# Input embedding projected directly behind the sums of the feed-forward norms, banks exchanged, and the third mixer's input split into a place of its own

## The chip, the core and the metric

The kernel runs on one core of a Trainium2 chip. The metric is the device time of one execution in microseconds (us). The core's engines are TensorE (PE, matmuls; its weight loads are listed as PEld), VectorE (DVE), ScalarE (ACT), GpSimd (POOL) and SyncE (SP, which here only issues DMAs). Each engine runs its own instructions in order and waits for others by semaphores.

## The reference

Two blocks follow each other on 512 tokens of width 1024. All is fp32. The first block has two layers; the second also has two (several small mixers, a gated merge), and the change touches it only by one wait. Of the first block:

```
for i in range(DEPTH):                       # DEPTH = 2
    y = mixer_ab(x, ...) if i % 2 == 0 else mixer_c(x, ...)
    x = layer_norm(ALPHA * x + y, ln_mix_g[i], ln_mix_b[i])
    f = conv_ffn(x, ffn_w_gate[i], ffn_w_up[i], ffn_conv_w[i], ffn_conv_b[i], ffn_w_down[i])
    x = layer_norm(ALPHA * x + f, ln_ffn_g[i], ln_ffn_b[i])
    x = x + jax.nn.sigmoid(x @ ple_w_gate[i]) * (p[i] @ ple_w_proj[i])
```

`conv_ffn` is `(gelu(conv3(x @ w_gate)) * (x @ w_up)) @ w_down` with an inner width of 2816 (22 tiles of 128). `p[i]` is a second input (an embedding) of width 256 for each layer; "embedding" below means it. `mixer_c` computes values, queries and keys from x and a differential attention.

## The kernel before, in words

**Layout.** Activations stand transposed: a tile is 128 features by 512 tokens, x has eight tiles. A matmul of fp32 precision is made of three passes of a faster type: each operand is split into `hi` (rounded) and `lo` (the rest), and the passes are hi*hi, hi*lo, lo*hi (function `passes`, L719 to L721). ACT (or DVE) makes `hi`, DVE makes `lo` (`upper`, `lower`); the split input of the projection at work stands in `moving`. Sums over features (norms) are fp32 matmuls with a matrix of ones (L924 to L937).

**Weights.** All weights come as 375 blocks of 128 x 1024 in a fixed order (`block_plan`). SP loads them into a ring of two slots, POOL splits each half block into `w_hi` and `w_lo` (L2526, L2529) as soon as PE has used the same half of the block two places before (`half_done`, `block_done`), and PE waits for `split_ready`. A block is 24 matmuls of 512 columns.

**Order.** The order of every engine is written out by hand: lists of stages (`mixer_a`, `heads_ab`, ..., `residual_norm`, `feed_forward`, `per_layer`, `mixer_c`, ...) that run alike on each engine. Norms are numbered i = 0 to 3; even ones follow a mixer, odd ones the feed-forward. Eight PSUM banks of 512 columns hold all results of PE; each stage has its banks by number.

**The steps that matter here.**
- Setup: DVE makes the angles for the rotary tables, ACT computes Sin of them (L1529 to L1531), and only then, in its `mixer_a`, copies the first values from banks 0 to 3 (L1434). PE's latent blocks go to the same banks and wait for these copies. ACT copies the latent blocks behind DVE's last setup step (L1541).
- A norm (`residual_norm` on PE, `norm_squares` on ACT, `residual`, `norm` on DVE): ACT squares each tile, DVE adds the squares (L2067, `add_squares`), PE sums mean (L927) and squares (L932). DVE centres four tiles (L2131) and POOL four (`recentre`, L2551); DVE scales each tile into a bank (L2160), ACT writes `hi` (L1609), DVE `lo` (L2137). At the end DVE computes x = hi + lo for all eight tiles (L2168).
- `feed_forward`: PE computes gate and up of the first tile pairwise as the normed tiles arrive, then tile by tile. DVE starts with the split of the embedding (`lower(("p", layer))`), then per tile two taps of the convolution (L2181, L2185), the product (L2190) and the `lo` of the hidden tile (L2195). Then PE computes the down projection in two halves, for which DVE and ACT have little to do.
- `per_layer`: PE projects the first half of the embedding (`project_p`, banks 4 to 7) when the four centred tiles and the mean are through with their banks, then the first two gate blocks pairwise as the normed tiles arrive, then gate blocks 2 to 7 to banks n % 4, and the embedding's second half in between. ACT takes the sigmoid (L1635), DVE multiplies in the bank (L2203) and adds to x (L2205). In layer 0 ACT and DVE then split all eight tiles of x into `moving` (L1429, L1842) for `mixer_c`; in layer 1 they make `gained` for the second block tile by tile.
- `mixer_c`: values of four 128-token groups in two halves (banks 0 to 3, then 4 to 7), then 16 query and key blocks in banks t % 4.

## Time and profile before

| | |
|---|---|
| median of 3 runs | 2528.85 us (2526.66 to 2528.97) |
| the profiled execution's own time | 2527.82 us |
| its span, first to last instruction | 2526.0 us |
| mean granted TensorE clock | 0.987 |
| PE busy | 2424.8 us (96%) |
| POOL busy | 1898.6 us (75%) |
| DVE busy | 1149.5 us (46%) |
| ACT busy | 690.9 us (27%) |
| weights and inputs read | 203.71 MB, 81 GB/s over the span |

Busy time is the time in which an engine had an instruction at work. Matmuls overlap each other, so their own durations (0.39 us) are longer than the distance of their starts. The granted clock is given in parts of full speed. In a timeline row stand the start, the duration, the engine, the line, the operation with out<-in, and in brackets how long the engine had been idle before and who released it; rows of equal instructions in a stretch are merged with their count.

### The profile page before, as it was taken

What the parts mean: (1) busy time and instruction counts of PE and PEld (TensorE: products, weight loads), DVE (VectorE), ACT (ScalarE), POOL (GpSimd) and SP (SyncE); (2) the same over time, 40 slices, a digit from 0 to 9 for tenths busy, and PEclk for the clock granted to TensorE, in tenths of its full rate; (3) what the DMA queues carried; (4) which work ended last, traced back from release to release, by engine and by line L of the source; (5) the groups of instructions that cost most, each with busy time, mean ns of one, the idle gap of its engine ahead of it and who ended that gap; (6) DMA issues with size and microseconds to landing.
All of it is one profiled execution on the core that took longest, in us unless ns stands there. A gap on an engine that the chain in (4) does not pass through costs nothing.

```text
span 2526.0 us, 32296 instructions
## 1 busy us (share of the span) xinstructions
PE 2424.8 (96%) x11118; PEld 1871.2 (74%) x11118; DVE 1149.5 (46%) x1587; ACT 690.9 (27%) x1242; POOL 1898.6 (75%) x1553
## 2 busy tenths in 40 slices
PE   7989989999999999899999999999999999999998
PEld 6755768888877843678888777767888877678886
DVE  6576563330261477643322474555322645553323
ACT  2166233330021157233320133144010231450101
POOL 8703578888877753698888799735999998359995
PEclk9999999999999999999999999999999999999999
DMA  4201122222222210122222232201222222112222
GB/s 175 84 9 43 51 75 100 98 93 100 92 75 100 85 41 1 67 100 91 100 97 95 75 113 100 84 34 59 100 97 94 92 100 85 41 53 99 99 99 84
DMA packets 57547, 207.11 MB, mean 82 GB/s; under 512 B 6512, under 2 KB 6896, under 8 KB 57200
## 3 DMA queue, kind: packets, MB, share of 16 engines
q1 hardware_dynamic: 55872, 199.87, 22.2%
q10 hardware_dynamic: 1584, 5.96, 0.6%
q8 instruction: 65, 1.06, 0.2%
q14 instruction: 26, 0.21, 0.0%
HBM read 203.71 MB, written 2.10 MB: 81 GB/s over the span
## 4 chain that ended last, share of the span: by engine, by line
PE 76%; DVE 10%; POOL 7%; issue 4%; ACT 2%; DMA 1%; POOLq 0%; DVEq 0%; ACTq 0%; SPq 0%
PE bank L719 21%; PE bank L721 20%; PE bank L720 20%; POOL w_hi L2526 4%; PE bank L813 4%; PE bank L768 3%; POOL w_lo L2529 3%; PE bank L841 2%; PE bank L867 2%; PE bank L888 1%; DVE branch_lo L1842 1%; DVE moving_lo L1842 1%; DVE x L2168 1%; DVE work L1882 1%; PE bank L906 1%
## 5 line engine op out<-in xcount | busy, mean ns | idle before, releaser
L2526 POOL TENSOR_TENSOR w_hi<-ring,unit 128x512 fp32r<-128x512 f32 x750 | 846.4, 1129 | 497.3 <-PE bank L721 357.0
L2529 POOL TENSOR_TENSOR w_lo<-ring,w_hi 128x512 fp32r<-128x512 f32 x750 | 1010.6, 1347 | 58.7
L719 PE MATMUL bank<-moving_hi,w_hi 128*128 128x512 f32 x1962 | 776.3, 396 | 26.8 <-DVE moving_lo L2137 12.3
L721 PE MATMUL bank<-moving_hi,w_lo 128*128 128x512 f32 x1962 | 768.8, 392 | 0.0
L720 PE MATMUL bank<-moving_lo,w_hi 128*128 128x512 f32 x1962 | 768.7, 392 | 0.0
L719 PEld LDWEIGHTS bank<-moving_hi,w_hi 128*128 128x128 f32 x1962 | 371.5, 189 | 116.9 <-issue 25.7
L720 PEld LDWEIGHTS bank<-moving_lo,w_hi 128*128 128x128 f32 x1962 | 371.4, 189 | 78.8 <-issue 1.9
L721 PEld LDWEIGHTS bank<-moving_hi,w_lo 128*128 128x128 f32 x1962 | 371.1, 189 | 78.4
L2473 DVE TENSOR_TENSOR region<-region,bank 128x512 f32<-128x512 f32 x64 | 39.7, 682 | 278.4 <-PE bank L721 278.4
L719 PE MATMUL bank<-hid_hi,w_hi 128*128 (+1 forms) x352 | 137.7, 391 | 0.0
L1780 ACT ACTIVATE region<-bank 128x512 f32<-128x512 f32 x64 | 38.1, 598 | 363.4 <-PE bank L721 363.4
L721 PE MATMUL bank<-hid_hi,w_lo 128*128 (+1 forms) x352 | 137.0, 389 | 0.0
L720 PE MATMUL bank<-hid_lo,w_hi 128*128 (+1 forms) x352 | 137.0, 389 | 0.0
L813 PE MATMUL bank<-region 64*128 64x512 f32 (+3 forms) x448 | 125.4, 574 | 11.8 <-ACT work L1496 3.0
L1903 DVE TENSOR_REDUCE negmax<-bank 128x2 f32<-128x256 f32 (+2 forms) x64 | 59.1, 924 | 112.6 <-PE bank L817 87.1
L2181 DVE SCALAR_TENSOR_TENSOR region<-bank,cols,region 128x511 f32<-128x511 f32 x44 | 32.9, 748 | 162.6 <-ACT region L1623 162.6
L1448 ACT ACTIVATE region<-bank 128x1024 f32<-128x1024 f32 (+2 forms) x80 | 66.7, 834 | 120.6 <-PE bank L867 120.4
L813 PEld LDWEIGHTS bank<-region 64*128 64x128 f32 (+1 forms) x448 | 40.1, 186 | 67.6 <-issue 46.5
L1599 ACT ACTIVATE region<-region 128x512 f32<-128x512 f32 x14 | 8.8, 631 | 265.5 <-DVE region L2059 183.6
L2091 DVE SCALAR_TENSOR_TENSOR region<-x,bank 128x512 f32<-128x512 f32 x18 | 12.2, 687 | 150.4 <-PE bank L721 150.2
L867 PE MATMUL bank<-tabs,work 128*128 128x128 f32 x496 | 69.5, 276 | 9.3 <-DVE work L1882 7.2
L867 PEld LDWEIGHTS bank<-tabs,work 128*128 128x128 f32 x496 | 53.9, 141 | 32.9 <-issue 25.8
(299 smaller groups left out, 3441.1 us busy)
## 6 DMA issues: line engine op xcount, KB each, us to landing
ring<-in_weights SPq DMA_DIRECT2D x375, 512.0 KB, 3.2
x<-in_x_t ACTq DMA_DIRECT2D x4, 512.0 KB, 8.4
out<-region SPq DMA_DIRECT2D x8, 256.0 KB, 2.2
region<-in_tables ACTq DMA_DIRECT2D x1, 1312.0 KB, 9.3
region<-in_tables ACTq DMA_DIRECT2D x1, 1024.0 KB, 5.7
region<-in_p_t ACTq DMA_DIRECT2D x2, 512.0 KB, 4.9
region<-in_tables SPq DMA_DIRECT2D x1, 320.0 KB, 10.4
small_w<-in_small_w ACTq DMA_DIRECT2D x1, 320.0 KB, 5.9
```

The lines of the kernel that those rows point to most:

```text
L719: pe.matmul(bank, lhs[0], rhs[0], start=start, stop=False, skip_group_check=True)
L720: pe.matmul(bank, lhs[0], rhs[1], start=False, stop=False, skip_group_check=True)
L721: return pe.matmul(bank, lhs[1], rhs[0], start=False, stop=stop, skip_group_check=True)
L768: mm = pe.matmul(bank, cols_of(w, k * P, P)[p == 2], moved(k)[p == 1], start=(j == 0), stop=(j == 23), skip_group_check=True)
L813: mm = pe.matmul(at[c], q(u, c)[:, i * P:i * P + P], k(u, c)[:, 0:w], start=True, stop=True)
L841: mm = pe.matmul(out_bank(u)[HD * c:HD * c + HD, 2 * P * h + lo:2 * P * h + 2 * P], v(u, t, c), pt_half[:, h, c, t, lo:2 * P], start=(open ...
L867: mm = pe.transpose(psum[4 + c][:, kt * P:kt * P + P], prob[:, 2 * (t % 2) + c, kt * P:kt * P + P], ident)
L1448: act.activation(pt_half[:, i // 2, :, 0:kt, lo:lo + P], banks[:, 4:6, 0:kt * P].rearrange("p c (k q) -> p c k q", k=kt), ACT.Copy).then_i ...
L1842: dve.tensor_tensor(pair[1], src, pair[0].bitcast(F32), ALU.subtract).then_inc(parts_ready, 1)
L1903: dve.tensor_reduce(negmax[:, at:at + 2], banks[:, b:b + 2, 0:w], AX_X, ALU.max, negate=True).then_inc(maxed, 2)
L2526: pool.tensor_tensor(w_parts[0][:, s, at], ring[:, s, at], unit[:, 0:1].broadcast_to([P, BLK // 2]), ALU.mult).then_inc(split_hi, 1)
L2529: pool.tensor_tensor(w_parts[1][:, s, at], ring[:, s, at], w_parts[0][:, s, at].bitcast(F32), ALU.subtract).then_inc(split_ready, 1)
```

## The change

It has these parts.
- ACT's four copies of the first values stand in `setup`, before the wait for DVE's angles.
- x = hi + lo becomes `join_parts`. Odd norms keep it at their end. Behind even norms it moves to the end of DVE's `feed_forward`, behind the last hidden tile, followed by the split of the embedding, which stood at its beginning. A new semaphore `x_joined` holds back ACT's scaled tiles and DVE's residual of the odd norm.
- Odd norms: DVE adds the squares of tiles 0 to 5; tiles 6 and 7 are added by PE with a matmul of their own each.
- `project_p` stands before the waits for the centred tiles; the embedding goes to banks 4, 6, 0, 1 (before 4 to 7) and the gate to 5, 7, 2, 3 (before 0 to 3). The gate pair also waits for the variance. The second block's first projection waits for the seventh finished tile of x (before: the fifth sigmoid).
- `mixer_c` reads `moving_c`, two places of 16 KB a partition in memory that is free then. In layer 0 ACT makes `hi` of tile n-1 behind the sigmoid of tile n, and DVE `lo` of tile n-1 behind the sum of tile n. The value halves use banks 4 to 7 first (when six tiles of x are finished) and 0 to 3 then; the first four query blocks use banks 6, 7, 2, 3.

```diff
+PLE_BANK, GATE_BANK = (4, 6, 0, 1), (5, 7, 2, 3)
+SQUARES_ODD = 6
+C_BANK = (6, 7, 2, 3) + (0, 1, 2, 3) * 3
...
+        moving_c = parts("moving_c", 32, KD, S)
...
             # PE, residual_norm
                 if i % 2:
-                    pe.wait_ge(square_added, T["square_added"][(i, KD - 1)])
-                mm = pe.matmul(psum[7][:], ones, square_sum, start=True, stop=(i % 2 == 1), skip_group_check=True)
-                if i % 2 == 0:
-                    pe.wait_ge(squared, T["squared"][("ln", i, KD - 1)])
-                    mm = pe.matmul(psum[7][:], ones, square_late[:, 3, :], start=False, stop=True, skip_group_check=True)
+                    pe.wait_ge(square_added, T["square_added"][(i, SQUARES_ODD - 1)])
+                pe.matmul(psum[7][:], ones, square_sum, start=True, stop=False, skip_group_check=True)
+                for n in range(SQUARES_ODD if i % 2 else KD - 1, KD):
+                    pe.wait_ge(squared, T["squared"][("ln", i, n)])
+                    mm = pe.matmul(psum[7][:], ones, square_late[:, n - 4, :], start=False, stop=(n == KD - 1),
+                                   skip_group_check=True)
...
             # PE, per_layer
+                        project_p(layer, 0)
                         pe.wait_ge(centered, CENTRED * (2 * layer + 2))
                         pe.wait_ge(drift_ready, 2 * layer + 2)
-                        project_p(layer, 0)
-                        project_pair(AT[("plegate", layer, 0)], (psum[0][:], psum[1][:]), ("ln", 2 * layer + 1))
+                        pe.wait_ge(variance, 2 * layer + 2)
+                        project_pair(AT[("plegate", layer, 0)], [psum[GATE_BANK[j]][:] for j in range(2)],
+                                     ("ln", 2 * layer + 1))
...
             # PE, mixer_c
-                    pe.wait_ge(x_ple, KD)
-                    tokens_values([("vC", 4 * half + i) for i in range(4)], moved,
-                                  [psum[4 * half + i][:] for i in range(4)], S, 2, ready=("x", 1))
+                    pe.wait_ge(x_ple, KD if half else KD - 2)
+                    tokens_values([("vC", 4 * half + i) for i in range(4)], moved_c,
+                                  [psum[4 * (1 - half) + i][:] for i in range(4)], S, 2, ready=("x", 1))
...
             # PE, project_second
-                    pe.wait_ge(ple_sig, KD * DEPTH - KD + 5)
+                    pe.wait_ge(x_ple, KD * DEPTH - KD + 7)
...
             # ACT, setup (and gone from mixer_a)
+                values(range(4), ("vA", 3), lambda i: v_ab[:, i, :], lambda i: psum[i])
                 act.wait_ge(setup_dve, SETUP["rest"])
...
             # ACT, per_layer
-                    if layer and n:
-                        gain(0, n - 1)
+                    if n:
+                        gain(0, n - 1) if layer else upper_x(n - 1)
...
-                    for n in range(KD):
-                        act.wait_ge(x_ple, n + 1)
-                        upper(("x", 1, n), moving[0][:, n, :], x[:, n, :])
+            def upper_x(n):
+                act.wait_ge(x_ple, n + 1)
+                upper(("x", 1, n), moving_c[0][:, n, :], x[:, n, :])
...
             # DVE, residual
-                    for n in range(4, KD):
+                    for n in range(4, SQUARES_ODD):
                         add_squares(i, n)
...
             # DVE, norm
-                dve.wait_ge(parts_ready, T["parts"][("ln", i, KD - 1)])
+                if i % 2:
+                    dve.wait_ge(parts_ready, T["parts"][("ln", i, KD - 1)])
+                    join_parts()
+
+            def join_parts():
                 for n in range(KD):
                     hi, lo = both(moving, np.s_[:, n, :])
-                    dve.tensor_tensor(x[:, n, :], hi.bitcast(F32), lo.bitcast(F32), ALU.add)
+                    ins = dve.tensor_tensor(x[:, n, :], hi.bitcast(F32), lo.bitcast(F32), ALU.add)
+                return ins
...
             # DVE, feed_forward
-                lower(("p", layer), both(p_parts, np.s_[:, :, :]), p_in_t)
                 with dve.Fori(0, KF // 2) as it:
...
+                join_parts().then_inc(x_joined, 1)
+                lower(("p", layer), both(p_parts, np.s_[:, :, :]), p_in_t)
...
             # DVE, per_layer
+                    if layer == 0 and n:
+                        lower_x(n - 1)
                 if layer:
                     last_gained(0)
-                for n in range(KD if layer == 0 else 0):
-                    lower(("x", 1, n), both(moving, np.s_[:, n, :]), x[:, n, :])
+                else:
+                    lower_x(KD - 1)
+
+            def lower_x(n):
+                lower(("x", 1, n), both(moving_c, np.s_[:, n, :]), x[:, n, :])
```

## Rows read from the trace of the kernel before

**Rows 1.** page, part 1: busy time (share of the span) and instructions of each engine

```profile
PE 2424.8 (96%) x11118; PEld 1871.2 (74%) x11118; DVE 1149.5 (46%) x1587; ACT 690.9 (27%) x1242; POOL 1898.6 (75%) x1553
```

**Rows 2.** waits of PE over the span: total, times, longest us

```profile
PE bank L719 <- DVE moving_lo L1842: 14.6, 4, 9.6
```

**Rows 3.** windows by stretch: length, busy of PE, PEld, DVE, ACT, POOL, granted clock, DMA

```profile
701.67:706.50 4.83, 4.83 (x12) 3.78 (x13) 4.60 (x8) 1.50 (x3) 0.00 (x0) 0.50 0.00 0
...
721.00:760.00 39.00, 38.73 (x167) 31.30 (x168) 14.52 (x18) 3.59 (x6) 37.75 (x32) 1.00 0.29 100
```

**Rows 4.** timeline of PE, first value block's end: start, us, engine, line, [idle before]

```profile
37.95 0.76 PE L719 MATMUL bank<-moving_hi,w_hi 128*128 128x512 f32 x1 [3.65 <-ACT region L1434]
...
44.84 0.39 PE L719 MATMUL bank<-moving_hi,w_hi 128*128 128x512 f32 x1
```

**Rows 5.** timeline of ACT, setup and first latent copy

```profile
33.75 0.63 ACT L1529 ACTIVATE rope_a<-region 128x512 f32<-128x512 f32 x1 [17.09 <-DVE region L1945]
...
46.83 0.60 ACT L1541 ACTIVATE region<-bank 128x512 f32<-128x512 f32 x1 [7.52 <-DVE cmp_bias_bf L1969]
```

**Rows 6.** timeline of POOL, setup

```profile
33.25 1.61 POOL L2529 TENSOR_TENSOR w_lo<-ring,w_hi 128x512 fp32r<-128x512 f32 x1
```

**Rows 7.** timeline of PE, start of the feed-forward behind norm 0

```profile
339.82 0.42 PE L719 MATMUL bank<-moving_hi,w_hi 128*128 128x512 f32 x1
...
353.36 0.49 PE L719 MATMUL bank<-moving_hi,w_hi 128*128 128x512 f32 x1 [1.22 <-DVE region L2190]
```

**Rows 8.** timeline of DVE, the same stretch and the down projection's end

```profile
336.34 11.57 DVE L2168 TENSOR_TENSOR x<-moving_hi,moving_lo 128x512 f32<-128x512 f32 x8
347.84 2.31 DVE L1842 TENSOR_TENSOR p_lo<-region,p_hi 128x1024 fp32r<-128x1024 f32 x1
...
631.11 1.29 DVE L2091 SCALAR_TENSOR_TENSOR region<-x,bank 128x512 f32<-128x512 f32 x2 [56.83 <-PE bank L721]
```

**Rows 9.** timeline of POOL: beside the sums, and in the down projection

```profile
339.58 1.49 POOL L2526 TENSOR_TENSOR w_hi<-ring,unit 128x512 fp32r<-128x512 f32 x1
341.15 1.63 POOL L2529 TENSOR_TENSOR w_lo<-ring,w_hi 128x512 fp32r<-128x512 f32 x1
...
560.43 1.04 POOL L2526 TENSOR_TENSOR w_hi<-ring,unit 128x512 fp32r<-128x512 f32 x1 [0.31 <-PE bank L721]
561.55 1.30 POOL L2529 TENSOR_TENSOR w_lo<-ring,w_hi 128x512 fp32r<-128x512 f32 x1
```

**Rows 10.** timeline of DVE, feed-forward norms 1 and 3

```profile
692.48 5.32 DVE L2067 TENSOR_TENSOR region<-region 128x512 f32<-128x512 f32 x4
...
703.25 1.42 DVE L2160 SCALAR_TENSOR_TENSOR bank<-region,cols,rstd 128x512 f32<-128x512 f32 x2
...
714.83 1.60 DVE L2137 SCALAR_TENSOR_TENSOR moving_lo<-bank,cols,moving_hi 128x512 fp32r<-128x512 f32 x2
...
1447.78 1.59 DVE L2137 SCALAR_TENSOR_TENSOR moving_lo<-bank,cols,moving_hi 128x512 fp32r<-128x512 f32 x2
```

**Rows 11.** timeline of PE, feed-forward norms 1 and 3

```profile
697.85 1.12 PE L932 MATMUL bank<-region,tabs 128*128 128x512 f32 x2 [2.58 <-DVE region L2067]
...
701.67 0.76 PE L719 MATMUL bank<-p_hi,w_hi 128*128 128x512 f32 x1 [2.69 <-issue]
...
709.87 0.47 PE L719 MATMUL bank<-moving_hi,w_hi 128*128 128x512 f32 x1 [0.20 <-POOL w_lo L2529]
...
730.16 0.39 PE L719 MATMUL bank<-moving_hi,w_hi 128*128 128x512 f32 x1
...
1463.89 0.39 PE L719 MATMUL bank<-moving_hi,w_hi 128*128 128x512 f32 x1
```

**Rows 12.** timeline of POOL, recentring in norm 1

```profile
695.98 5.40 POOL L2551 TENSOR_TENSOR region<-region 128x512 f32<-128x512 f32 x4 [1.35 <-ACT region L1601]
```

**Rows 13.** timeline of PE, first value block of the third mixer

```profile
764.20 0.52 PE L719 MATMUL bank<-w_hi,moving_hi 128*128 128x512 f32 x1 [3.77 <-DVE moving_lo L1842]
...
767.92 0.39 PE L719 MATMUL bank<-w_hi,moving_hi 128*128 128x512 f32 x1
```

35 lines of the change are left out of this document (21 added, 14 removed).

## The prediction, written before the changed kernel was run

> **What bounds the kernel now.** The first part of the page has TensorE (PE) busy 96% of the span [rows 1]: the matmuls set the end, and a change pays only where PE stands still or runs slowly. So I read next where PE stood (the waits of PE over the span, then PE's timeline around each wait). PE's largest releaser is the DVE split into `moving_lo`: 14.6 us in four waits, one of them inside the part that changes [rows 2]. A stop costs more than its length: behind the stop of 697.85 to 701.67 the granted clock is 0.50 (the 1.2 GHz level) for 4.83 us, while in 721 to 760 it is 1.00 (2.4 GHz) [rows 3]. At full clock matmuls start 0.227 us apart (0.68 for the three passes), at half clock 0.427; a block of 24 is 5.44 us of PE. GpSimd (POOL) splits each half block in about 2.4 us when alone, 2.72 us of PE each; it is the second bound wherever it starts late.
>
> **Change 1, the first value copies ahead of the Sin work.** Before, PE stands 3.65 us from 34.30 to 37.95, and reaches the next block at 44.84, 6.89 us later for 5.44 us of work, since the first matmuls are cold [rows 4]. ACT sat 17.09 us waiting for DVE's angles, ran Sin, and only then copied [rows 5]. With the copies first, they start at 34.34, and one takes 0.60 us (as the ACT copy at 46.83 [rows 5]), so the first ends at about 34.95 and PE starts at 35.1. The weights' first half is split at 34.86 [rows 6], so that is no bound. A gap of 0.95 us I take as harmless: behind the 1.22 us gap of [rows 7] the next matmuls are at full pace. PE reaches the next block at 35.1 + 5.44 = 40.6; POOL's next two halves, 2.4 to 3.1 each [rows 9], are there at 39.7 to 41.1. I take 40.7: gain 44.84 - 40.7 = **4.1**. Price: Sin starts at 36.6 + 1.3 (table load) instead of 33.75, so DVE's tables end some 4 us later and ACT's first latent copy moves from 46.83 [rows 5] to about 50.7; PE needs it only at the fifth latent block, 35.1 + 4 x 5.44 = 56.9. Bounds: 4.9 (the whole stop and its cold part) and 2.5 (POOL, already the pace here, meets DVE's moved work and gives 1.6 of it back).
>
> **Change 2, the sum x = hi + lo leaves the start of the feed-forward.** Behind norms 0 and 2 DVE runs the eight sums (11.57 us) and the split of p (2.31 us) before its first convolution step [rows 8]. That does two things to PE: it reaches the third tile only at 353.36 behind DVE's late product, and POOL's halves stretch to 3.14 us (1.49 + 1.62 and the gaps) against 2.42 alone [rows 9], which stops PE for 0.3 to 0.4 us three times. From 339.82 to 353.36 are 13.54 us for 48 matmuls, 10.88 at full pace [rows 7]: 2.66 lost. Without the sums the first product is there at 344.9 (341.6 when ACT's first tap ends, two taps 1.8, Gelu 0.65, product 0.7) and PE asks for it at 350.7; POOL's halves fit. Norm 2 has the same rows. Gain 2 x 2.66 = **5.3**; below, 2 x 1.2 (the DVE wait alone).
> The sums now run behind DVE's last hidden tile, in the down projection, where DVE idles 56.83 us before the residual [rows 8] and POOL waits for PE 0.31 us before each half [rows 9]. With two slots of two halves, POOL finishes a half 3 x 2.72 - 2.42 = 5.7 us ahead of its need. 13.9 us of sums and split delay it by 4.4 halves x (3.14 - 2.72) = 1.9 us, under 5.7: cost 0. ACT's scaled tiles and DVE's residual wait for it, both needed some 40 us later. If that lead were gone, 2 x 1.9.
> The Trainium skill (SBUF — State Buffer, Who interferes with whom) has the port between DVE and GpSimd as an exclusive lock, also for a DVE instruction with two SBUF inputs: the second to come fully blocks. The sums have two SBUF inputs and both engines do stretch, but POOL by 0.45 and 0.33 us a piece, not by a whole DVE instruction of 0.65. By the rule taken whole, POOL would lose 9 to 10 x 0.65 = 6.5 us in the down projection, 0.8 more than its lead, and the sum would be 1.6 us smaller.
>
> **Change 3, feed-forward norms (1 and 3).** Of DVE's four adds of squares (5.32 us [rows 10]) two go to PE as two more matmuls of 0.9 us. The squares' sum then follows the mean's matmuls at 695.3 without the 2.58 us stop [rows 11] and ends at 698.0 instead of 698.95, so the norm's chain comes 0.9 earlier. `project_p` no longer waits for centring (its stop of 2.69, named issue, ends 0.1 behind DVE's last centre): it runs from 698.0 to 703.6, warm, in place of 701.67 to 709.5. POOL's four recentres end at 701.4 [rows 12] and its next half at 704.1, so the pair of gates starts with the first normed tile at 704.6. Now DVE paces it: its chain from the first scaled tile to the last `moving_lo` is 13.2 us (703.25 to 716.43) at norm 1 and 12.3 at norm 3 (ending 1449.37) [rows 10]; with 0.9 off and 0.4 to 0.6 on (POOL now splits beside the last tiles) the last is ready at 715.9 and 1449.1, and PE is through 1.6 us later, at 717.5 and 1450.6, where before it was at 709.87 + 48 x 0.227 = 720.8 and at 1455.2. Then POOL is the pace for three halves, since its first half can start only behind the sixth tile, and the sums stand beside more of them. By halves of 3.14 PE reaches the fourth gate's second half at 726.2 and 1459.05, before at 730.16 and 1463.89 [rows 11]: gains 3.9 and 4.8, **8.7**. Above: 5.8 each (2.7 stop, 2.0 cold, 0.9, 0.2). Below: 2 each, the cold part alone; the clock rival goes under that.
>
> **Change 4, third mixer's input to its own place.** The splits could not start before the last gate block had read `moving`; PE stood 3.77 us and ran nine matmuls cold [rows 13]. Its fourth group of three starts at 767.92; at full pace it would have been there at 762.3 (764.20 less 3.77 of stop and 0.16 of drain, and three groups of 0.68): 5.6. Now seven of eight tiles are split under the gate blocks. The last block ends at 760.2; tile 7 takes sigmoid, product, sum, hi, lo: about 4 us, and is asked for by the fourth value block, 16.3 us later. The first half of the values also waits for six finished tiles (banks 4 to 7); the sixth is 5 us old by then. Gain **5.6**; below 3, if ACT's order (hi of tile n-1 between two sigmoids) delays a sigmoid. Each `lower` has two SBUF inputs and costs POOL 0.35 to 0.45; per block POOL has 5.44 - 4.8 = 0.6 to spare, just enough: **-0.3** at the start, where it has no lead (0 to -1). The wait of layer 1's first projection moves from the fifth sigmoid to the seventh finished tile, about 3 us before PE is there: 0. The exchanged banks of the queries wait for copies that are ten microseconds old: 0.
>
> **Sum.** 4.1 + 5.3 + 8.7 + 5.6 - 0.3 = 23.4 us. The profiled execution took 2527.8 (span 2526.0), within the measured 2526.7 to 2529.0 and 1 below the median: 2527.8 - 23.4 = 2504.4.
>
> **Rivals.**
> A, the freed time goes to the port: POOL, starting at once behind the recentres, meets every DVE step of the norm, and at each norm the tile-paced pair gives back 1 us and the three halves behind it 2; the start gives back 1.6, mixer C 2: 9.6 together, gain 13.8, 2514. For: POOL is the releaser in [rows 11] already. Against: the same two halves stood beside the same tiles before, only later.
> B, slower: the clock stays low through the norms. In place of one long stop PE now has many short ones, and a stop of 2.58 and one of 2.69 with 1.12 of work between [rows 11] brought it to 0.50 [rows 3]. If projection and pair (72 matmuls) run at 0.427 us, they end at 698.0 + 10.2 + 20.5 = 728.7, 7.9 behind before, at both norms: -15.8 instead of +8.7, total -1.1 (2528.9); each further cold matmul adds 0.2, and with 20 of them the loss is over 0.2%. It decides if the pair's gaps (1.45 to 1.7 us a tile for 1.36 us of work) are enough to lower the clock. Against: in 339 to 353 PE stopped 0.3 to 1.2 us four times and the starts keep 0.23.
> The Trainium skill (TensorE: Matmul & The Clock Gate, A second HAM failure mode: psum-queue depth-cycling) reports just this, short idle times between groups of matmuls making the clock swing. By that rule the pairs would run between the levels; rival B is its full price, half of it 2516.
> C, mixer C's stop is only moved: a wait for the sixth or eighth finished tile ends late and the clock falls again. Gain 17.8, 2510.
>
> **Chances.** Forecast with its own spread 0.72, A 0.12, C 0.08, B in part (2514 to 2524) 0.05, B whole 0.03. 0.2% is 5 us, what this measurement can tell from no change. Faster 0.95, same 0.03, slower 0.02. The terms' bounds give gains up to 27.6 (2500) and down to 10 to 14 (2514); the range for 8 in 10 is 2499 to 2513.
>
> **What would show it.** No PE wait of 3.65 near 34; the third tile of each feed-forward without a wait for DVE's product, and the `x` sums some 40 us before the residual, with no PE wait beside them; six instead of two instructions in the squares' sum, `p_hi` matmuls right behind at clock 1.00; PE waits of 0.1 to 0.4 us on `moving_lo` of the norm in the pair; no wait and clock 1.00 at the first value block of mixer C. Wrong: clock 0.5 in the pair (B), waits on `w_lo` over 3 us more than before (A), a wait over 1 us at mixer C's start (C).

## The result and the profile after

The changed kernel takes 2511.9 us (median of 6 runs, 2511.1 to 2514.5) where the kernel before takes 2529.4 (6 runs, 2526.7 to 2530.9): a ratio of 0.9935, 95% interval 0.9924 to 0.9945, so 0.55 to 0.76% faster. The forecast was 2504.4, its range 2499 to 2513. The profiled execution of the changed kernel has a span of 2511.0 against 2526.0: 15.0 us less, where the forecast counted 23.4.

The first part of the page: TensorE does the same work, and eight matmuls more for the squares, in a shorter span [rows 1].

```profile
span 2511.0 us, 32310 instructions
PE 2426.7 (97%) x11126; PEld 1874.6 (75%) x11126; DVE 1164.7 (46%) x1583; ACT 691.3 (28%) x1242; POOL 1899.4 (76%) x1553
```

The waits of PE over the whole span:

```profile
PE bank L724 <- DVE moving_lo L2153: 17.4, 4, 6.2
PE bank L724 <- DVE moving_lo L1856: 10.9, 3, 9.7
...
PE bank L724 <- DVE x L2228: 1.6, 1, 1.6
```

Of a wait, the profile gives the total, the number and the longest one. The four waits for `moving_lo` that were 14.6 us [rows 2] are three and 10.9: mixer C's is gone. But the split inside the norms (12.3 us in two waits before, norms 0 and 2) now stops PE four times, and the wait for `x` is new. PE's timeline at the places of [rows 4, 7, 11, 13]:

```profile
35.19 0.47 PE L724 MATMUL bank<-moving_hi,w_hi 128*128 128x512 f32 x1 [0.73 <-ACT region L1443]
40.74 0.39 PE L724 MATMUL bank<-moving_hi,w_hi 128*128 128x512 f32 x1
...
348.40 0.39 PE L724 MATMUL bank<-moving_hi,w_hi 128*128 128x512 f32 x1
...
692.44 0.79 PE L724 MATMUL bank<-p_hi,w_hi 128*128 128x512 f32 x1
...
701.15 0.47 PE L724 MATMUL bank<-moving_hi,w_hi 128*128 128x512 f32 x1 [2.55 <-DVE moving_lo L2153]
...
704.75 0.51 PE L724 MATMUL bank<-moving_hi,w_hi 128*128 128x512 f32 x1
...
723.58 0.40 PE L724 MATMUL bank<-moving_hi,w_hi 128*128 128x512 f32 x1
...
755.26 0.39 PE L724 MATMUL bank<-w_hi,moving_c_hi 128*128 128x512 f32 x1
...
1446.94 0.40 PE L724 MATMUL bank<-moving_hi,w_hi 128*128 128x512 f32 x1
...
1456.37 0.50 PE L724 MATMUL bank<-p_hi,w_hi 128*128 128x512 f32 x1 [1.62 <-DVE x L2228]
...
1483.61 0.50 PE L724 MATMUL bank<-gained_hi,w_hi 128*128 128x512 f32 x1 [0.27 <-DVE gained_lo L2304]
```

Both kernels issue the same 2834 groups of three passes in the same order, so the n-th group of one can be set against the n-th of the other. How far the changed kernel is ahead at each: 4.1 us at 40.74 (before 44.84, [rows 4]), 5.0 at 348.40 (353.36, [rows 7]), 5.1 at the end of the down projection, 7.3 at 723.58, 12.7 at 755.26 (767.92, [rows 13]), 15.5 behind the next feed-forward's start, 17.6 at 1446.94, 16.0 at 1456.37, 15.1 near the end. The difference of two such numbers is what a stretch gained, whatever happened ahead of it. By it the start gave 4.2, the two feed-forward starts with the norms ahead of them 2.1 and 1.9 (the part behind the pair of gates 2.7 each time), norms 1 and 3 gave 2.2 and 2.1, mixer C 5.6. The wait for `x` took 1.7, and stretches that nobody had edited took 1.1 (heads A, the first mixer's attention) and gave 1.0 (heads C, the third mixer's). The second block took 0.8. Of that, 0.5 stands at 1483.61, where its first projection now waits for DVE's `gained_lo`; the forecast had priced this place at 0.

The same division is used for every run below. Each number is how much later (+) or earlier (-) the stretch ends than in the changed kernel, its own start taken off; the last column is the sum over the whole kernel, with the stretches that the table leaves out.

| kernel | norm 0 and start of gates | norm 1 | second `p`, layer 0 | mixer C start | heads C | norm 2 and start of gates | norm 3 | second `p`, layer 1 | all |
|---|---|---|---|---|---|---|---|---|---|
| before | +2.1 | +2.2 | -0.2 | +5.6 | +1.0 | +1.9 | +2.1 | -1.7 | +15.1 |
| e14 changed again | -0.1 | 0.0 | 0.0 | 0.0 | 0.0 | 0.0 | 0.0 | 0.0 | -0.3 |
| e1 POOL holds | -0.4 | +0.4 | -0.2 | 0.0 | +0.9 | -0.7 | +1.2 | -1.7 | -1.7 |
| e2 project_p late | -0.3 | -1.0 | 0.0 | 0.0 | 0.0 | -1.3 | +0.4 | -1.9 | -4.2 |
| e3 kept busy | -0.7 | -1.3 | +1.8 | 0.0 | +0.9 | -1.1 | -1.3 | +3.1 | -2.0 |
| e4 sums split | -0.1 | -0.7 | +0.1 | 0.0 | 0.0 | -1.3 | -1.7 | -0.6 | -3.9 |
| e6 sums back | +1.8 | -1.3 | +1.8 | 0.0 | +1.7 | +1.5 | -1.3 | +3.1 | +6.8 |
| e7 late and split | 0.0 | -1.7 | +0.1 | 0.0 | +1.7 | -0.1 | -1.8 | -0.7 | -2.2 |
| e9 mixer C back | -0.2 | 0.0 | 0.0 | +6.9 | +0.1 | -0.1 | 0.0 | 0.0 | +6.3 |
| e10 squares back | 0.0 | +0.7 | 0.0 | 0.0 | +0.9 | -0.7 | -1.0 | +3.1 | +2.0 |
| e11 neither | -0.8 | +1.9 | -0.2 | 0.0 | 0.0 | -1.1 | +1.9 | -1.9 | -1.4 |
| e12 late, even busy | -2.1 | +0.7 | -0.2 | 0.0 | 0.0 | -2.3 | +1.2 | -1.7 | -7.4 |
| e13 late, all busy | -2.1 | -1.0 | 0.0 | 0.0 | +1.7 | -2.3 | -1.0 | 0.0 | -5.3 |

The two profiled executions of the changed kernel (the first and e14, 2512.8 and 2512.5 us) differ by 0.1 at most in each stretch. Different kernels differ by 0.7 to 1.3 at norm 2 and by 0.9 or 1.7 in heads C though nothing was edited there, and by up to 3.0 in the second block, which the table leaves out (e3 and e12 gained 3.0 and 2.8 there): that much is not the edits' doing. Each row is also one execution of several. Those of e7 and e6 that were profiled took 2510.6 and 2519.6, about 3 and 2 us more than most of their others; e12's, at 2505.5, took 2 to 3.6 less than its others. So a row tells where that execution gained or lost, and its last column is no better measure of a kernel than the median.

**What stands at norm 1 now.** DVE's timeline, then POOL's:

```profile
697.29 3.06 DVE L2176 SCALAR_TENSOR_TENSOR bank<-region,cols,rstd 128x512 f32<-128x512 f32 x2
700.27 0.74 DVE L2153 SCALAR_TENSOR_TENSOR moving_lo<-bank,cols,moving_hi 128x512 fp32r<-128x512 f32 x1
...
710.82 12.46 DVE L2188 TENSOR_TENSOR x<-moving_hi,moving_lo 128x512 f32<-128x512 f32 x8
```

```profile
695.94 1.04 POOL L2554 TENSOR_TENSOR w_hi<-ring,unit 128x512 fp32r<-128x512 f32 x1
697.06 1.29 POOL L2557 TENSOR_TENSOR w_lo<-ring,w_hi 128x512 fp32r<-128x512 f32 x1
698.68 1.12 POOL L2554 TENSOR_TENSOR w_hi<-ring,unit 128x512 fp32r<-128x512 f32 x1 [0.33 <-PE bank L726]
699.88 1.60 POOL L2557 TENSOR_TENSOR w_lo<-ring,w_hi 128x512 fp32r<-128x512 f32 x1
```

DVE's first two scaled tiles took 3.06 us where they had taken 1.42 [rows 10]. The granted clock behind the stop of 698.60 to 701.15 (the columns are those of [rows 3], the last but two the clock):

```profile
702.00:704.00 2.00, 2.00 (x6) 1.54 (x6) 1.97 (x4) 1.18 (x2) 0.00 (x0) 0.50 0.65 223
704.00:706.00 2.00, 2.00 (x8) 1.63 (x7) 1.93 (x4) 0.89 (x2) 0.00 (x0) 0.75 0.10 39
```

The pair's first nine matmuls take 3.60 us (701.15 to 704.75) instead of 9 x 0.227 = 2.04; seven of them start 0.43 apart. ("Cold" below means matmuls at the lower of the two clock levels, granted clock 0.50, 1.2 GHz; "warm" means 1.00, 2.4 GHz.) Not all of these 1.6 us are the clock's. In e6 below, the same pair starts behind the same stop and stays warm, and its first nine take 2.40 (702.78 to 705.18): the clock costs 1.2. At the end of the pair the changed kernel has gained 2.1 us, where the forecast had 3.3 (717.5 against 720.8). With the pair warm it is 2.9 (e3 and e6).

**The sums behind norm 3.** Before, and now:

```profile
1449.41 7.69 DVE L2168 TENSOR_TENSOR x<-moving_hi,moving_lo 128x512 f32<-128x512 f32 x8
```

```profile
1434.17 12.46 DVE L2188 TENSOR_TENSOR x<-moving_hi,moving_lo 128x512 f32<-128x512 f32 x8
```

With the lead of 15.5 us added, the changed kernel's start in the same place (1449.7), but take 4.8 us more, since POOL now splits beside every one of them: a sum takes 0.69 us alone and 1.34 to 1.77 there. The finished tiles of `x` stand behind them. Among the kernels with eight sums in a row, PE waits for `x` in layer 1 exactly where the sums took 12.5 to 12.6 (the changed kernel, e3, e6, e9, e10, e13, e14) and nowhere that they took 7.7 or 9.6 (before, e1, e2, e11, e12).

### The profile page after: what moved, and what is told of

It is laid out like the page before. It is cut to its first block, busy times and chain, and to the rows that moved or that the text cites. A ratio compares the mean times of both kernels' runs of the same rounds, so it can differ in the third digit from the quotient of the medians.

```text
span 2511.0 us, 32310 instructions
## 1 busy us (share of the span) xinstructions
PE 2426.7 (97%) x11126; PEld 1874.6 (75%) x11126; DVE 1164.7 (46%) x1583; ACT 691.3 (28%) x1242; POOL 1899.4 (76%) x1553
## 4 chain that ended last, share of the span: by engine, by line
PE 81%; DVE 9%; POOL 5%; issue 3%; ACT 1%; DMA 0%; POOLq 0%; DVEq 0%; ACTq 0%
PE bank L724 22%; PE bank L726 22%; PE bank L725 22%; PE bank L818 4%; PE bank L773 3%; POOL w_hi L2554 3%; POOL w_lo L2557 2%; PE bank L846 2%; PE bank L872 2%; PE bank L893 1%; DVE branch_lo L1856 1%; DVE work L1896 1%; PE bank L911 1%; DVE negmax L1917 1%; ACT region L1707 0%
## 5 line engine op out<-in xcount | busy, mean ns | idle before, releaser
L724 PE MATMUL bank<-moving_hi,w_hi 128*128 128x512 f32 x1834 | 728.6, 397 | 24.1 <-DVE moving_lo L2153 17.4
L725 PE MATMUL bank<-moving_lo,w_hi 128*128 128x512 f32 x1834 | 721.5, 393 | 0.0
L726 PE MATMUL bank<-moving_hi,w_lo 128*128 128x512 f32 x1834 | 721.4, 393 | 0.0
L724 PEld LDWEIGHTS bank<-moving_hi,w_hi 128*128 128x128 f32 x1834 | 348.9, 190 | 106.8 <-issue 27.6
L725 PEld LDWEIGHTS bank<-moving_lo,w_hi 128*128 128x128 f32 x1834 | 349.1, 190 | 74.5 <-issue 1.9
L726 PEld LDWEIGHTS bank<-moving_hi,w_lo 128*128 128x128 f32 x1834 | 348.7, 190 | 73.9
L1469 ACT ACTIVATE work<-bank,negmax 128x512 f32<-128x512 f32 (+3 forms) x128 | 71.3, 565 | 24.7 <-DVE negmax L1917 24.7
L2215 DVE TENSOR_TENSOR hid_lo<-region,hid_hi 128x512 f32 x44 | 58.6, 1331 | 40.9 <-ACT hid_hi L1642 40.9
```

What stands on the lines that cost most here:

```text
L724: pe.matmul(bank, lhs[0], rhs[0], start=start, stop=False, skip_group_check=True)
L725: pe.matmul(bank, lhs[0], rhs[1], start=False, stop=False, skip_group_check=True)
L726: return pe.matmul(bank, lhs[1], rhs[0], start=False, stop=stop, skip_group_check=True)
L1469: act.activation(p, p if masked else psum[2 * (t % 2) + c][:, 0:w], ACT.Exp, bias=negmax[:, at:at + 1], scale=-1.0 if masked else 1.0, acc ...
L2215: dve.tensor_tensor(hid[1][:, tile, :], gelu_t[:, par, :], hid[0][:, tile, :].bitcast(F32), ALU.subtract).then_inc(hid_parts, 1)
```

## The experiments

Medians are of all runs of a kernel; before, in the same turns, was at 2527.6 to 2529.6 in the four sets.

### e1: is it POOL that holds DVE's first scaled tiles?

```diff
                 for n in range(CENTRED, KD):
                     pool.tensor_tensor(tiles[:, n, :], tiles[:, n, :], drift, ALU.subtract).then_inc(recentered, 1)
+                if i % 2:
+                    pool.wait_ge(normed, T["normed"][("ln", i, 1)])
```

> The changed kernel, but in norms 1 and 3 POOL waits, behind its four recentres, until DVE's first two scaled tiles are out, instead of splitting the next half block at once. Theory (the port): the two scaled tiles took 3.06 us instead of 1.42 because they stood behind POOL's w_lo and w_hi splits; with POOL still they take 1.4 us again and the first moving_lo is ready 1.5 us earlier. PE gains next to nothing by it (0 to 0.5 us a norm), since its pair then waits for POOL's half, which comes at 698.8 + 2.4 = 701.2 instead: the wait ahead of the pair stays 2.5 us and changes its releaser from DVE to POOL. Rival (PSUM or PE): the tiles are slow because PE's matmuls of project_p write other banks at the same time; then they still take 3 us with POOL still, and the pair starts about where it did.

Measured: 2511.1 us (one run). DVE's, POOL's and PE's timeline at norm 1 of this kernel:

```profile
696.11 1.42 DVE L2176 SCALAR_TENSOR_TENSOR bank<-region,cols,rstd 128x512 f32<-128x512 f32 x2
```

```profile
697.61 1.04 POOL L2554 TENSOR_TENSOR w_hi<-ring,unit 128x512 fp32r<-128x512 f32 x1 [2.86 <-DVE bank L2176]
```

```profile
700.57 0.77 PE L724 MATMUL bank<-moving_hi,w_hi 128*128 128x512 f32 x1 [3.15 <-POOL w_lo L2557]
```

With POOL still, the two tiles take 1.42 us, while `project_p` runs on PE as before: POOL's splits are the cause, PE is not. The prediction of [rows 9] counted this lock at 0.33 to 0.45 us a piece on POOL's side; here DVE, the engine that came second, lost 1.64 us in two instructions. The Trainium skill (SBUF — State Buffer, Who interferes with whom) has the second one fully blocked; this trace agrees: the first tile, issued at 697.29, comes out only at 698.91, behind POOL's `w_lo` (697.06 to 698.35). As expected the pair gains nothing by it, since PE then waits for POOL. At norm 3 fourteen matmuls then ran cold (+1.2 in the table), but the eight sums took 7.70 us instead of 12.46, and the wait for `x` was gone (-1.7).

### e2: the projection late again

```diff
-                        project_p(layer, 0)
                         pe.wait_ge(centered, CENTRED * (2 * layer + 2))
                         pe.wait_ge(drift_ready, 2 * layer + 2)
                         pe.wait_ge(variance, 2 * layer + 2)
+                        project_p(layer, 0)
```

> The changed kernel, but project_p in norms 1 and 3 stands behind the waits for centring, drift and variance again; banks, squares on PE and the rest stay. Theory: PE stops about 3.3 us from 692.4 to 695.7 instead of 2.55 at 698.5, project_p runs at the 1.2 GHz level and is through at about 704, the pair at 715, where the changed kernel had 713.6; POOL's next halves come later too. So 1.4 to 2 us a norm slower than the changed kernel, 3 to 4 in all: 2515. In other words the early projection is worth 1.5 to 2 us a norm, not the 3 to 4 that the prediction needs from it. Rival (the prediction's price): it is worth 3 us or more a norm, and what failed is something else: 2518 or more. Second rival: the stop is only moved and it is worth nothing: 2512.

Measured: 2509.3 us (2507.1 to 2509.9, 4 runs), ratio to before 0.9922 (0.9905 to 0.9938). All three theories missed: undoing the step makes the kernel faster than the changed one, by 2.7 us in the medians. The two starts at norm 1, and norm 3's:

```profile
695.34 0.47 PE L724 MATMUL bank<-p_hi,w_hi 128*128 128x512 f32 x1 [2.69 <-DVE region L2147]
...
701.36 0.47 PE L724 MATMUL bank<-moving_hi,w_hi 128*128 128x512 f32 x1 [0.20 <-POOL w_lo L2557]
...
1416.39 0.47 PE L724 MATMUL bank<-p_hi,w_hi 128*128 128x512 f32 x1 [2.69 <-DVE region L2147]
...
1418.42 0.63 PE L725 MATMUL bank<-p_lo,w_hi 128*128 128x512 f32 x1
...
1423.75 0.47 PE L724 MATMUL bank<-moving_hi,w_hi 128*128 128x512 f32 x1
```

The pair starts at 701.36, where it was 701.15 in the changed kernel (0.6 later, with the lead of 0.4 that this execution has ahead of the norm), though `project_p` starts 2.9 us later (695.34 against 692.44): what sets the pair's start is the norm's chain and POOL's half, not where `project_p` stands. PE stops once either way, for 2.55 or 2.69 us. But late, the stop lies ahead of `project_p`, and cold matmuls, where there are any (norm 3, 1418 to 1421), fall at least in part into time in which the pair could not have run. Early, it lies ahead of the pair, and the cold matmuls there are paid. POOL's next half, too, is split later (698.52), behind DVE's first two tiles, which take 1.42 us.

The table says how much of the gain this is. Of 2.4 us in the four stretches of change 3, norm 1 gives 1.0 and norm 3 loses 0.4. The other 1.9 is at the second `p` of layer 1, where the sums took 9.63 us and nobody waited for `x`. e4 and e7 below settle what is left without that wait: both have the sums cut in two and none for `x`, and late projection (e7) is ahead of early (e4) by 1.2 us in the four stretches, 1.0 of it at norm 1. Their ratios to before, 0.9918 and 0.9919, do not tell them apart.

### e3: PE kept busy in the stop

```diff
+            def keep_busy(first, bank, count):
+                half_of(first, 0)
+                w = w_parts[0][:, first % RING, :]
+                for _ in range(count):
+                    pe.matmul(bank, w[:, 0:P], w[:, 0:S], start=True, stop=True, skip_group_check=True)
...
                         pe.wait_ge(variance, 2 * layer + 2)
+                        keep_busy(AT[("plegate", layer, 0)], psum[5][:], 10)
```

> The changed kernel, with ten more matmuls of 512 columns behind project_p in norms 1 and 3, into a bank that the pair then overwrites; they fill the 2.55 us in which PE stood. Theory (the clock): the stop itself can't be shortened so, since the first normed tile comes at 701.0 either way, but the nine matmuls behind it no longer run at 0.43 us: 1.5 us less for the pair, which then follows DVE's tiles and is through at 712.2 instead of 713.6, and POOL's halves behind it start 1.5 us earlier. 1.2 to 1.5 us a norm, 2.4 to 3 in all: 2509. Rival: the pair is paced by DVE and POOL anyway, so that the colder clock costs nothing: 2512, with clock 1.00 in the pair and new waits of the same sum in it. Second rival: the extra matmuls come too late and delay the pair: slower than 2512.

Measured: 2512.6 us (2510.8 to 2513.9, 4 runs), ratio 0.9938 (0.9921 to 0.9954): no faster than the changed kernel. PE's starts at norms 1 and 3:

```profile
699.91 0.47 PE L724 MATMUL bank<-moving_hi,w_hi 128*128 128x512 f32 x1 [0.29 <-DVE moving_lo L2160]
...
730.47 0.50 PE L724 MATMUL bank<-p_hi,w_hi 128*128 128x512 f32 x1 [1.26 <-DVE x L2235]
...
1455.77 0.50 PE L724 MATMUL bank<-p_hi,w_hi 128*128 128x512 f32 x1 [2.82 <-DVE x L2235]
```

The clock is what made the pair slow: warm, each norm ends 1.3 us earlier, as the first theory has it. e6 shows the same gain at both norms without any filling, since there the stop of 2.55 was followed by full clock. It is given back and more at the next thing that DVE owes: the second projection of `p` waits for the fourth finished tile of `x`, which stands behind the eight sums. That wait, in layer 1 with eight cold matmuls behind it, costs 1.8 and 3.1 us. None of the theories had it there. (That the profiled execution, the fastest of the four, is 2.0 us shorter than the changed kernel all the same comes from the second block, which gave 3.0.)

### e4: the sums behind norms 1 and 3 cut in two

```diff
-                    join_parts()
+                    join_parts(range(4))
...
                 for n in range(KD):
+                    if n == 4:
+                        join_parts(range(4, KD))
                     dve.wait_ge(ple_sig, KD * layer + n + 1)
```

> The changed kernel, but the eight sums x = hi + lo behind norms 1 and 3 are cut in two: tiles 0 to 3 directly behind the norm, tiles 4 to 7 ahead of the per-layer term of tile 4. Theory: in the changed kernel they end at 723.2 and 1446.6, the finished tiles 0 to 3 come behind them, and the second projection of p in layer 1 waits 1.62 us for the fourth. With four sums less ahead it comes some 4 us earlier and that wait is gone: 1.6 us less, 2510; nothing changes in layer 0, where nobody waited. Rival: sums in the midst of the gate blocks make the tiles 4 to 7 late, so that mixer C's first block or layer 1's kcvc waits by as much: 2512 with a new wait there, or slower.

Measured: 2508.8 us (2506.9 to 2509.4, 4 runs), ratio 0.9919 (0.9902 to 0.9935). The wait for `x` is gone:

```profile
710.61 6.21 DVE L2188 TENSOR_TENSOR x<-moving_hi,moving_lo 128x512 f32<-128x512 f32 x4
...
728.34 6.37 DVE L2188 TENSOR_TENSOR x<-moving_hi,moving_lo 128x512 f32<-128x512 f32 x4
```

Four sums instead of eight stand ahead of the finished tiles. That is 3.1 us less, twice what was expected. The wait's own stretch gained 0.6 net (1.8 up to it, 1.2 given back behind it, where the other four sums now stand). Behind the pairs of gates PE was 0.7 and 0.8 us faster; fewer sums stand beside POOL's halves there. The rest, 0.9 in norm 3's pair, which ran warm behind its stop of 2.56, and 1.3 at norm 2, is not the edit's.

### e6 and e9: changes 2 and 4 undone, one at a time

```diff
-                if i % 2:
-                    dve.wait_ge(parts_ready, T["parts"][("ln", i, KD - 1)])
-                    join_parts()
+                dve.wait_ge(parts_ready, T["parts"][("ln", i, KD - 1)])
+                ins = join_parts()
+                if i % 2 == 0:
+                    ins.then_inc(x_joined, 1)
...
+                lower(("p", layer), both(p_parts, np.s_[:, :, :]), p_in_t)
                 with dve.Fori(0, KF // 2) as it:
...
-                join_parts().then_inc(x_joined, 1)
-                lower(("p", layer), both(p_parts, np.s_[:, :, :]), p_in_t)
```

> The changed kernel with change 2 alone undone: the eight sums x = hi + lo and the split of p stand at the start of each feed-forward again. Theory: the sums cost 2.6 us at each of the two starts, as the traces before and after show between the pair of gates and the fourth tile, and nothing in the down projection, so 5.1 to 5.3 us slower than the changed kernel: 2517. Rival: part of that came from the other changes or is given back in the down projection (POOL's lead there), and undoing it costs under 3 us: below 2515.

```diff
-        moving_c = parts("moving_c", 32, KD, S)
+        moving_c = moving
...
-                        gain(0, n - 1) if layer else upper_x(n - 1)
+                        gain(0, n - 1) if layer else None
...
-                    upper_x(KD - 1)
+                    for n in range(KD):
+                        upper_x(n)
...
-                    if layer == 0 and n:
-                        lower_x(n - 1)
...
-                    lower_x(KD - 1)
+                    for n in range(KD):
+                        lower_x(n)
```

> The changed kernel with change 4 alone undone in what matters: mixer C's input shares its place with the gates' input again, and both of its parts are made for all eight tiles behind the last gate block; the banks stay exchanged. Theory: the stop of 3.8 us and its cold matmuls come back at mixer C's first value block, 5.4 us slower than the changed kernel: 2517.3. Rival: the splits under the gate blocks cost POOL and DVE something that then comes back as a gain: under 4 us slower, below 2516.

Measured: e6 2517.7 us (2517.3 to 2519.9, 5 runs), ratio 0.9960 (0.9946 to 0.9975), so 5.8 slower than the changed kernel, as its theory said. But the stretches put only 1.8 and 1.5 of it at the two feed-forward starts. The rest came at the second `p` (+1.8 and +3.1, the wait for `x` again), less 1.3 at each of norms 1 and 3, and 1.7 in heads C, which no edit touches. The sum was right; the expected place holds half of it, and for the rest the agreement is luck. The 1.3 at norms 1 and 3 is worth a look, for nothing was edited there. The stop ahead of the pair is as long as in the changed kernel, but the clock behind it stays full:

```profile
702.78 0.47 PE L724 MATMUL bank<-moving_hi,w_hi 128*128 128x512 f32 x1 [2.55 <-DVE moving_lo L2153]
```

```profile
702.00:704.00 2.00, 1.22 (x5) 1.05 (x6) 1.96 (x3) 0.99 (x2) 1.10 (x1) 1.00 0.00 0
```

e9 2519.1 us (2516.9 to 2521.6, 5 runs), ratio 0.9965 (0.9951 to 0.9979): 7.2 slower where 5.4 was expected, and by the stretches all of it where it was expected:

```profile
757.22 0.77 PE L724 MATMUL bank<-w_hi,moving_hi 128*128 128x512 f32 x1 [4.25 <-DVE moving_lo L1857]
```

The stop is longer than the old one (4.25 against 3.77 [rows 13]) and the stretch costs 6.9 where it had cost 5.6.

### e10 and e11: the other two corners of change 3

```diff
-SQUARES_ODD = 6
+SQUARES_ODD = KD
...
-                pe.matmul(psum[7][:], ones, square_sum, start=True, stop=False, skip_group_check=True)
+                mm = pe.matmul(psum[7][:], ones, square_sum, start=True, stop=(i % 2 == 1), skip_group_check=True)
```

> The changed kernel with the last two squares of norms 1 and 3 added by DVE again; project_p stays ahead of the waits for centring. Together with the run that had it the other way round (squares on PE, project_p late: 2509.3) and the kernels before and after this makes a table of two by two. New theory, from that run: the gain at these norms is the squares' alone, because they take away one of two stops that follow each other, and with them the low clock; the early projection only moves the remaining stop from before itself to behind itself, where it is followed by cold matmuls. Then this kernel loses nearly all of the norms' gain: PE stops 2.6 us for the squares, then 2.5 or more for the first normed tile, 3 to 4 us a norm slower than the changed kernel less what the early projection is worth: 2516 to 2519. The prediction's price: the squares are worth 0.9 us a norm, so 2513.8.

e11 has this and the edit of e2 together.

> The changed kernel with change 3 undone in both of its parts (the last two squares of norms 1 and 3 added by DVE again, and project_p behind the waits for centring); the exchanged banks stay. It closes the table: squares on PE alone 2509.3, early projection alone 2514.8, both 2511.9. Theory from the traces (the norms gave 2.3 and 2.2 us, less the new wait of 1.6 for x): the pair of edits was worth 3 us, so this is at 2515, which makes the early projection worth nothing without the squares and a loss of 2.7 with them, and the squares worth 5.5 where project_p is late. The prediction's price: change 3 worth 8.7, so 2520. Rival: the two are additive, so that this is 2514.8 - 2.7 = 2512.

Measured: e10 2514.8 us (2512.5 to 2514.8, 4 runs), ratio 0.9944 (0.9928 to 0.9961); e11 2511.4 (2511.3 to 2511.5, 4 runs), ratio 0.9933 (0.9918 to 0.9948).

| us, median (the four stretches of change 3, against the changed kernel) | `project_p` late | `project_p` early |
|---|---|---|
| last two squares on DVE | 2511.4 (+1.7) | 2514.8 (+2.8) |
| last two squares on PE | 2509.3 (-2.4) | 2511.9 (0) |

The four kernels were not run in the same turns, and the intervals of their ratios overlap. The runs of the late and the early kernels do not, and both ways of counting say the same of the order: early projection costs (3.3 and 2.7 us in the medians, 1.1 and 2.4 in the stretches), squares on PE gain (2.2 and 2.8, or 4.1 and 2.8). For e10 the theory had 2516 to 2519 and the prediction's price 2513.8; neither was met, the price came nearer. The rival of e11, that the two add up, came true; the theory's 2515 and the prediction's price (2520) did not. The medians have change 3 as a whole at nothing (-0.5), the stretches at +1.7; e11 was 1.1 earlier at norm 2 and 1.3 in the second block, which it does not edit.

Where early projection loses is not where e10's theory had it. With the squares on DVE, e10 is ahead of e11 by 1.2 us at norm 1 and by 2.9 at norm 3, and loses 5.0 at the second `p` of layer 1, behind 12.59 us of sums against 9.63. So there the early projection does shorten both norms, and the wait for `x` takes more than it gives.

e10's theory also needed the two stops in a row to bring the low clock. It falls at its own norm 1:

```profile
693.00 1.13 PE L937 MATMUL bank<-region,tabs 128*128 128x512 f32 x2 [2.58 <-DVE region L2081]
...
702.26 0.77 PE L724 MATMUL bank<-moving_hi,w_hi 128*128 128x512 f32 x1 [2.54 <-DVE moving_lo L2153]
```

```profile
694.00:696.00 2.00, 2.00 (x10) 1.64 (x9) 1.77 (x3) 0.73 (x1) 2.00 (x3) 1.00 0.00 0
...
702.00:704.00 2.00, 1.74 (x4) 1.48 (x5) 1.93 (x4) 0.87 (x2) 0.58 (x1) 0.50 0.20 35
```

Full clock behind the stop for the squares, half behind the one for the first tile. At its norm 3 it was the other way round: 0.65 and 0.50 from 1418 to 1422, behind the stop of 2.58 for the squares, and 1.00 behind a stop of 0.74 ahead of the pair.

### e7, e12, e13, e14: a version that beats both

e7 is e2 and e4 together.

> The changed kernel with project_p behind the waits for centring, and the sums behind norms 1 and 3 cut in two (tiles 4 to 7 ahead of the per-layer term of tile 4): the two edits that each came out at 2509. Theory: each took away the wait of the second projection of p for DVE's x in layer 1 (1.6 us), so the two share that; what is left of the split is 0.5 to 0.9 us at each norm, from sums that no longer stand beside POOL's halves: 2507.5. Rival, full sum of both: 2506. Second rival: the split adds nothing where project_p is late: 2509.2.

Measured: 2507.6 us (2507.3 to 2510.6, 4 runs), ratio 0.9918 (0.9902 to 0.9935), as its theory said. In the four stretches it is the best of all (-4.1). The profiled execution is the slowest of the four, 3 us above the others, and lost 1.7 in heads C. e12 is e2 with PE kept busy at norms 0 and 2, e13 is e12 with ten more such matmuls ahead of the wait for centring:

```diff
                 pe.wait_ge(hid_ready, KF * layer + 1)
+                keep_busy(n0, psum[0][:], 24)
                 project_pair(n0, (psum[0][:], psum[2][:]), ("ln", i - 1))
...
+                        keep_busy(AT[("pleproj", layer, 0)], psum[0][:], 10)
                         pe.wait_ge(centered, CENTRED * (2 * layer + 2))
```

> A version meant to beat both: the changed kernel with project_p behind the waits for centring (2509.3 by itself), and in norms 0 and 2 24 more matmuls of 512 columns in the 6.2 us in which PE waits for the first normed tile, into a bank that the pair then overwrites. Theory: behind that stop the clock is 0.50 for 5.5 us, some thirteen matmuls at 0.43 us, 2.6 us lost each time; kept busy, PE follows DVE's tiles (the last moving_lo is out at 333.3, so the pair ends at 334.7 instead of 337.4) and nothing behind it is short: 2 to 2.6 us a norm, 4 to 5 in all, 2505. Rival: as at norms 1 and 3, where a warm pair ran into the next bound and kept 0.8 of 2.4 us, DVE or POOL takes most of it back: 2508.

> The run before (project_p late, norms 0 and 2 kept busy) with ten more matmuls of 512 columns in the 2.7 us in which PE waits for centring at norms 1 and 3, ahead of project_p. There the same stop of 2.69 us has been followed by full clock in one kernel (694 to 704 at 1.00 with project_p late alone) and by the low one in others, so that norm 1 gave back 1.6 of the 2.3 us that norm 0 had gained. Theory: it's the clock; kept busy, project_p runs at 0.23 us a matmul each time, POOL's next half is freed up to 2 us earlier and the pair starts 1 to 1.9 us earlier at each of the two norms: 2505.5. Rival: the start of the pair is set by DVE's first tile and POOL's half anyway, and a cold project_p costs nothing since it falls into the time in which the pair could not run: 2508, with new waits of PE ahead of the pair as long as the cold matmuls were.

> The changed kernel as it is, once more on the same chip and in the same turns as the version that is to beat it. Both theories expect 2511.9, as measured the first time; a result 2 us or more away would say that the table of two by two, whose entries lie 2.5 us apart, can't be read from medians alone.

Measured: e12 2508.1 us (2505.5 to 2509.1, 5 runs), ratio 0.9921 (0.9908 to 0.9935). Norms 0 and 2 gave 2.1 and 2.3 us, as expected, but norms 1 and 3 came out 1.7 and 0.8 worse than in e2: behind the same stop of 2.69 us `project_p` now ran cold. The rival's 2508 was met, though not by its reason. (Its profiled execution, at 2505.5 the fastest of the five, had 2.8 us of its lead in the second block.) e13 2506.8 (2505.0 to 2507.5, 4 runs), ratio 0.9906 (0.9891 to 0.9921); e14, in the same turns, 2512.3 (2511.8 to 2512.5, 5 runs), as in its first six runs. e13 lies between its theory (2505.5) and its rival (2508). It has the lowest median of all, 5.5 us below the changed kernel and 22.8 below the kernel before; its runs overlap with those of e12 and e7. PE's starts in e13:

```profile
693.18 0.50 PE L724 MATMUL bank<-p_hi,w_hi 128*128 128x512 f32 x1 [0.35 <-DVE region L2155]
...
699.23 0.47 PE L724 MATMUL bank<-moving_hi,w_hi 128*128 128x512 f32 x1 [0.19 <-POOL w_lo L2565]
...
1451.26 0.50 PE L724 MATMUL bank<-p_hi,w_hi 128*128 128x512 f32 x1 [1.58 <-DVE x L2236]
```

Against e12 the pair's start moved from 701.03 to 699.23 and from 1423.79 to 1421.00, so a cold `project_p` is not wholly free: POOL's half waits for it. In e12, then in e13:

```profile
698.19 1.04 POOL L2561 TENSOR_TENSOR w_hi<-ring,unit 128x512 fp32r<-128x512 f32 x1 [4.58 <-PE bank L726]
```

```profile
696.39 1.04 POOL L2562 TENSOR_TENSOR w_hi<-ring,unit 128x512 fp32r<-128x512 f32 x1 [2.95 <-PE bank L726]
```
The wait for `x` is back at 1451.26, and e4's split would be the next thing to try on top of e13; it was not run.

## Why the prediction was right, and where its sum was not

The sign, the range and three of four mechanisms held; the gain was 15.0 to 17.5 us (profiled spans, medians) instead of 23.4. The range held by 1.1 us at its slow end, which is less than stretches that no edit touches moved from kernel to kernel, so that it held at all is in part luck.

**Change 1** was priced at 4.1 and gave 4.2: PE starts at 35.19 (forecast 35.1) and reaches the next block at 40.74 (forecast 40.7), full clock behind a stop of 0.73. ACT's first latent copy came at 49.34 (50.7) and nobody waited for it. The 1.1 us lost in heads A afterwards has no step of the change in it; its cause is not shown.

**Change 2** was priced at 5.3. Behind the pair of gates it gave 2.7 twice, the third tile has no wait, and the eight sums in the down projection (12.65 us) cost nothing: the lead stayed at 5.07 through it.

```profile
569.14 12.65 DVE L2188 TENSOR_TENSOR x<-moving_hi,moving_lo 128x512 f32<-128x512 f32 x8
```

Undone alone it cost 1.8 and 1.5 there. The cold stretch at norms 0 and 2 took 0.7 and 0.9 back, which the sum did not have.

**Change 4** was priced at 5.6 - 0.3 and gave 5.6; no wait, no cold matmul at 755.26. Undone, it costs 6.9. Rival C is out. The wait of the second block's first projection, priced at 0, cost 0.5.

**Change 3** is the step that failed: 8.7 forecast (3.9 and 4.8), 2.2 and 2.1 found, less 1.7 for the wait for `x`. Three things in its working were wrong.
- "The pair of gates starts with the first normed tile at 704.6": the norm's chain did come 0.9 earlier, but the tile came 1.6 late (701.15 + 5.1 = 706.2), because POOL, freed early by the early projection, held DVE's first two tiles (e1). Little of these 1.6 us is seen at the end of the pair, which DVE paces: with the clock full it lacks only 0.4 of the forecast (2.9 against 3.3). The forecast had looked for POOL slowing the tiles by 0.4 to 0.6 in all.
- "Now DVE paces it": the stop of 2.55 us had only moved from ahead of `project_p` to ahead of the pair, and with it, in this kernel, the cold matmuls. Kept busy (e3), or where the clock stayed full by itself (e6), the norm is 1.3 shorter. That is part of rival B, at 1.3 us a norm instead of 7.9; the forecast gave the clock no price at all here, though [rows 3] showed one behind two such stops.
- What the fourth finished tile of `x` costs stood in no term. The forecast priced what the sums beside POOL cost POOL, and not what they cost DVE: norm 3 ends 2 us earlier, DVE's sums start no earlier and take 12.46 us instead of 7.69, and the second projection of `p` waits 1.62 us. Further gains at the norm met it again (e3, e6, e10: 2.8 us).

So within change 3 the half meant to bring most, the early projection, is a loss of 2.4 us by the stretches, of which 1.9 is at the wait for `x` and 0.5 at the norms themselves. The squares, priced at 0.9 a norm, are worth 1.4 to 2.0 by the stretches and 1.1 to 1.4 by the medians. Rival A had the right mechanism (the port) at the right place for part of this, and its total, 2514, lies 2 us above the result, where the forecast lies 7.5 below; its three halves of POOL were not what it cost.

Left open: why heads A, heads C and the second block differ by up to 3 us between kernels that issue the same work there, what of the result beyond 15.0 (the medians have 17.5) they make up, and what decides whether the clock falls behind a stop of 2.55 us.

## What to carry to other kernels

When the start of a stage is set by another engine's chain, filling the wait with other work need not shorten it. It can move the stop to directly ahead of the stage, where cold matmuls, if the clock falls, are paid. Try such work on both sides of the stop, or fill the stop as well. When a step is moved earlier, ask which engine it frees and what that engine will then hold up, here DVE's first tiles and its eight sums. Then look one wait further for the next thing that the faster engine is owed: most of the loss stood there.

## What the runs showed of the hardware that was not expected

- The same stop of 2.69 us ahead of `project_p` was followed by full clock in one kernel and by the low level in others. In e2, and then in e11, both at norm 1:

```profile
694.00:696.00 2.00, 0.66 (x3) 0.60 (x4) 1.97 (x5) 0.20 (x1) 1.50 (x2) 1.00 0.00 0
696.00:698.00 2.00, 2.00 (x11) 1.59 (x10) 1.93 (x4) 0.28 (x1) 0.00 (x0) 1.00 0.00 0
```

```profile
696.00:698.00 2.00, 1.94 (x5) 1.58 (x6) 1.90 (x4) 0.00 (x0) 0.00 (x0) 0.50 0.00 0
698.00:700.00 2.00, 2.00 (x6) 1.56 (x5) 1.87 (x4) 1.35 (x2) 0.00 (x0) 0.50 0.00 0
```

  e11 had a second stop of 2.58 us just ahead, but e12 had not and ran cold too. At norm 3 of e12 fourteen matmuls of `project_p` ran cold, 1414.99 to 1421.0, 2.8 us lost; in e2's norm 3 eight. The stop of 2.55 or 2.56 directly ahead of the pair was followed by cold matmuls in the changed kernel, e9, e14 (norms 1 and 3) and e4 (norm 1), and by none in e6 (both) and e4 (norm 3). So what a single stop of about 2.6 us costs lies between nothing and 2.8 us, and one profile doesn't tell.
- Two profiled executions of the changed kernel stay within 0.1 us of each other in each stretch of the table, while other programs differ by 1 us or more at places that nobody edited. That is not proof that a program repeats itself so closely: these two took 2512.8 and 2512.5 us, all executions of this kernel 2511.1 to 2514.5, those of the kernel before 2525.3 to 2532.1, and no second profile shows where such executions differ.
- A split of POOL, once under way, held DVE's scaled tile (two inputs in SBUF) until it ended, twice in a row at both norms: 3.06 us for two tiles instead of 1.42. In the other direction POOL's pieces grew by 0.33 to 0.45 us only [rows 9]. DVE's sums beside them took 1.34 to 1.77 us instead of 0.69 each, so eight in a row took 7.7 to 12.6 us with the number of splits beside them.
